# Products of constants ahead of TensorE's waits in a two-block transformer kernel

## The reference, cut to what matters

```
def first_block(x, c, ...):
    for i in range(2):
        sh1, sc1, g1, sh2, sc2, g2 = split(silu(c) @ ada_w[i] + ada_b[i], 6)
        h = rms_norm(x, norm_mix[i]) * (1 + sc1) + sh1
        x = x + g1 * (mla_mixer(h, ...) if i == 0 else gdn_mixer(h, ...))
        h = rms_norm(x, norm_ffn[i]) * (1 + sc2) + sh2
        x = x + g2 * (swiglu_ffn(h, ...) if i == 0 else moe_ffn(h, ...))
    return rms_norm(x, final_norm)

def second_block(x, ...):
    proj = rms_norm(x, norm_mix_pre) @ w_in
    ys = stack([rwkv7(proj), dilated_attention(proj), diff_attention(proj), conformer_conv(proj)])
    merged = sum_n(sigmoid(p_gate + gate_bias)[n] * (ys[n] @ w_branch[n]))
    x = x + rms_norm(merged @ w_out, norm_mix_post)
    h = rms_norm(x, norm_ffn_pre)
    return x + rms_norm((silu(h @ ffn_w_gate) * (h @ ffn_w_up)) @ ffn_w_down, norm_ffn_post)
```

## Time and profile before

| | |
|---|---|
| median of three runs | 3054.39 us |
| the profiled execution | 3055.6 us, its span 3054.3 us |
| TensorE busy | 2842.9 us (93%) |
| VectorE, ScalarE, GpSimd busy | 1724.3, 1246.3, 249.7 us |
| mean granted clock of TensorE | 0.973 |
| DMA | 387.94 MB, mean 127 GB/s |

### The profile page before, as it was taken

How to read it: one execution, slowest core, us unless ns; L and a number is a source line. 1 busy time by engine, 2 the same in 40 slices (tenths; PEclk the granted TensorE clock), 3 DMA queues, 4 the chain that set the end, 5 groups by cost and what they waited for, 6 DMA issues and landing times. The chain is left out here.

```text
span 3054.3 us, 40668 instructions
## 1 busy us (share of the span) xinstructions
PE 2842.9 (93%) x16535; PEld 2425.1 (79%) x16535; DVE 1724.3 (56%) x2989; ACT 1246.3 (41%) x2250; POOL 249.7 (8%) x224
## 2 busy tenths in 40 slices
PE   5988899999997989889999999899999999899998
PEld 4766788787886878789999997688778866678886
DVE  6666554445774867543468887543324396654344
ACT  2455432223433344423457776432223355432222
POOL 0000000000002543020000001112100002100000
PEclk8889999999999999989999999999999999999999
DMA  5232234422232111053579997211231203412321
GB/s 221 76 109 102 97 145 172 148 111 93 89 125 76 56 42 56 23 210 119 172 258 354 350 336 284 72 67 46 84 126 51 83 33 132 146 69 81 118 81 66
DMA packets 74418, 387.94 MB, mean 127 GB/s; under 512 B 8490, under 2 KB 10190, under 8 KB 42574
## 3 DMA queue, kind: packets, MB, share of 16 engines
q1 hardware_dynamic: 60816, 349.20, 31.3%
q10 hardware_dynamic: 10382, 26.07, 2.5%
q0 software_dynamic: 3024, 9.98, 0.9%
HBM read 368.43 MB, written 22.03 MB: 128 GB/s over the span
## 5 line engine op out<-in xcount | busy, mean ns | idle before, releaser
L342 DVE TENSOR_TENSOR wlo<-stage,whi 128x1024 fp32r<-128x1024 f32 (+4 forms) x524 | 533.8, 1059 | 352.2 <-ACT whi L354 351.6
L354 ACT ACTIVATE whi<-stage 128x1024 fp32r<-128x1024 f32 (+4 forms) x524 | 443.8, 896 | 210.7 <-PE ps L638 170.8
L638 PE MATMUL ps<-whi,mxhi 128*128 128x256 f32 x968 | 282.4, 292 | 11.0 <-DVE wlo L342 6.4
L638 PE MATMUL ps<-whi,mxlo 128*128 128x256 f32 x968 | 275.3, 284 | 0.0
L638 PE MATMUL ps<-wlo,mxhi 128*128 128x256 f32 x968 | 275.1, 284 | 0.0
L638 PE MATMUL ps<-bxhi,whi 128*128 128x512 f32 x480 | 199.7, 416 | 17.1 <-DVE bxlo L342 8.4
L638 PEld LDWEIGHTS ps<-whi,mxhi 128*128 128x128 f32 x968 | 186.5, 193 | 13.7 <-DVE wlo L342 5.6
L638 PE MATMUL ps<-bxhi,wlo 128*128 128x512 f32 x480 | 189.0, 394 | 0.0
L638 PE MATMUL ps<-bxlo,whi 128*128 128x512 f32 x480 | 188.5, 393 | 0.0
L638 PEld LDWEIGHTS ps<-wlo,mxhi 128*128 128x128 f32 x968 | 187.1, 193 | 0.0
L638 PEld LDWEIGHTS ps<-whi,mxlo 128*128 128x128 f32 x968 | 186.8, 193 | 0.0
(11 more groups left out here) (591 smaller groups left out, 6551.5 us busy)
## 6 DMA issues: line engine op xcount, KB each, us to landing
stage<-in_gu SPq DMA_DIRECT2D x91, 1024.0 KB, 5.8
more<-in_gu SPq DMA_DIRECT2D x41, 1024.0 KB, 7.0
stage<-in_ada SPq DMA_DIRECT2D x40, 1024.0 KB, 4.9
stage<-in_dn SPq DMA_DIRECT2D x36, 768.0 KB, 5.3
stage<-in_dn SPq DMA_DIRECT2D x32, 640.0 KB, 5.0
stage<-in_gin SPq DMA_DIRECT2D x16, 1024.0 KB, 4.8
stage<-in_gt SPq DMA_DIRECT2D x16, 1024.0 KB, 4.7
more<-in_dn SPq DMA_DIRECT2D x16, 640.0 KB, 5.1
```

What stands on the lines that cost most here:

```text
L342: return e.do.tensor_tensor(out, x, y, op)
L354: return e.do.activation(out, x, f, **kw)
L638: return self.p.do.matmul(out, lhsT, rhs, start=start, stop=stop, skip_group_check=True)
```

## The change

A new method `warm(n)` issues `n` plain fp32 products of the constant `ones` with the first 512 columns of the constants, into the bank that comes next in turn (after its last reader is done). Nobody reads them: the next real product into that bank starts a new sum. They are put ahead of 37 places in the executed program, 164 products in all. `pe_total` gets `ahead` and `behind`. At the query norm the wait for the whole table of constants moves ahead of the sum. The table `WARM` names heads and stages of the delta rule. `xs2`, `xs3`, `xs4`, `xs5` and `w2sum` are the sums of the norms ahead of the FFN, the delta rule, routing, the second block and that block's FFN.

```
+    def warm(self, n):
+        at = self.rot[self.turn % len(self.rot)]
+        before, self.prev[at] = self.prev[at], None
+        if before:
+            self.p.wait_ge(*[s(free(before)) for s in (self.A, self.V) if s.has(free(before))])
+        for _ in range(n):
+            self.mm(self.ps[at][:, :], self.c("ones"), self.cst_all[:, 0:512])
...
-    def pe_total(self, use, src, mark, ones=None, more=None):
+    def pe_total(self, use, src, mark, ones=None, more=None, ahead=0, behind=0):
+        self.warm(ahead)
...
         z.then_inc(*self.P.up(use))
+        self.warm(behind)
...
-        self.pe_total("sumq", L.tmp[0], V(("win", "sum", 3)))
         p.wait_ge(self.Dc("cst"))
+        self.pe_total("sumq", L.tmp[0], V(("win", "sum", 3)), ahead=9)
...
+        self.warm(6)
         for _ in self.pe_gemm("wo", "wo", range(4), L.X, lambda q: [V(("ot", "l", q))]):
...
+        self.pe_total("xs2", self.sq, self.V(("wo", "t", 6)), more=self.last_square, ahead=2, behind=8)
...
+        self.pe_total("xs3", self.sq, self.V(("f0", "t", 6)), more=self.last_square, ahead=3, behind=8)
...
+        self.warm(1)
         ps, vacant = self.take("bat")
...
+        self.warm(4)
         ps, vacant = self.take("gsum")
         p.wait_ge(self.V("decay"), *vacant)
         self.mm(ps[:, 0:32], self.c("tri"), L.sm(1))
         self.mm(ps[:, 32:64], self.c("ones"), L.sm(1)).then_inc(*P_.up("gsum"))
+        self.warm(5)
...
+    WARM = {(0, 2): 2, (0, 3): 7, (0, 4): 2, (1, 3): 3, (0, 6): 4, (0, 8): 4, (4, 3): 5, (4, 5): 3, (4, 8): 3, (3, 23): 4, (7, 26): 6}
...
+                self.warm(self.WARM.get((h, st), 0))
                 if st == 1:
...
+        self.pe_total("xs4", self.sq, V(("go", "t", 6)), more=self.last_square, ahead=2)
...
         for m in range(5):
+            self.warm(2)
             turn(m)
+        self.warm(3)
         ps, vacant = self.take("ranks")
...
         for m in range(5, 8):
             turn(m)
+        self.warm(7)
         self.pe_came(L, 0)
...
+        self.warm(8)
         self.pe_came(L, 1)
+        self.warm(2)
         gather(0, slice(0, 1))
         for t in range(2, tiles[0]):
             self.pe_came(L, t)
+        self.warm(3)
...
                         gather(0, slice(t, t + 1))
+                        self.warm((0, 1, 6, 1)[t])
...
+        self.pe_total("xs5", self.sq, self.V(("mo", "t", 6)), more=self.last_square, ahead=2, behind=18)
...
+        self.pe_total("w2sum", M.ring[0], self.V(("w2", "t", 6)), more=(M.ring[2], self.A(("w2", "q", 7))), ahead=3, behind=10)
```

More of the change, by code:

```diff
@@ L1324, in ffn0_pe @@
     def ffn0_pe(self, L, sums):
-        self.pe_total("xs2", self.sq, self.V(("wo", "t", 6)), more=self.last_square)
+        self.pe_total("xs2", self.sq, self.V(("wo", "t", 6)), more=self.last_square, ahead=2, behind=8)
         def between(e, j):
@@ L1511, in gdn_in_pe @@
         p, P_, A = self.p, self.P, self.A
-        self.pe_total("xs3", self.sq, self.V(("f0", "t", 6)), more=self.last_square)
+        self.pe_total("xs3", self.sq, self.V(("f0", "t", 6)), more=self.last_square, ahead=3, behind=8)
         for k, _ in enumerate(self.pe_gemm("gin", "gin", range(16), L.X, self.normed("n3"), lead=2)):
@@ L2055, in route_pe @@
         blocks = [slice(c * P, (c + 1) * P) for c in range(4)]
-        self.pe_total("xs4", self.sq, V(("go", "t", 6)), more=self.last_square)
+        self.pe_total("xs4", self.sq, V(("go", "t", 6)), more=self.last_square, ahead=2)
         for m in (5, 6, 7):
@@ L2652, in middle_pe @@
         self.p.wait_ge(*self.fence)
-        self.pe_total("xs5", self.sq, self.V(("mo", "t", 6)), more=self.last_square)
+        self.pe_total("xs5", self.sq, self.V(("mo", "t", 6)), more=self.last_square, ahead=2, behind=18)
     def middle_act(self, L):
@@ L3215, in merge_pe @@
             pass
-        self.pe_total("w2sum", M.ring[0], self.V(("w2", "t", 6)), more=(M.ring[2], self.A(("w2", "q", 7))))
+        self.pe_total("w2sum", M.ring[0], self.V(("w2", "t", 6)), more=(M.ring[2], self.A(("w2", "q", 7))), ahead=3, behind=10)
     def merge_act(self, L, M):
```

5 lines of the change are left out of this document (added).

## The result

The changed kernel takes 3095.57 us (median of 4, 3093.47 to 3097.15), the kernel before 3055.16 beside it (median of 4, 3051.13 to 3060.26): a ratio of 1.0134, 95% interval [1.0117, 1.0151]. The prediction had the direction right; its 3078 was 17 us short, and the time lies 3.6 us above the end of the wide range (3050 to 3092) and 5.6 above that of the forecast's own (3066 to 3090).

The account below looks back on a forecast made before the run. TensorE, busy 2842.9 of 3054.3 us, was taken to bound the kernel. Outside routing, 42.1 us of overruns less 22.4 of clock and 4 of later waits gave +15.7; routing +7.0; from 3055.6 to 3078, range 3066 to 3090 (wide 3050 to 3092).

Parts of the forecast that it names:

- A: Query norm: nine products ahead of the query sum, where no wait stands; 7.7 us overrun.
- B: Output projection: 6 products, 5.1 us, against a wait of 3.60 + 0.17; 1.35 us over.
- I: Second block's norm: 3 products ahead of its sum and 10 behind; 0.8 and 3.4 us over.
- C: FFN's norm: 2 products ahead fit their wait, 8 behind overrun theirs by 2.9 us.
- H: Branches' norm: 2 products ahead of the sum, 1.5 us over; 18 behind, 6.8 us over.
- D: Delta rule's norm: 3 products ahead about fill their wait, 8 behind overrun by 2.9 us.
- F: Delta rule's rounds: 12.2 us overruns, including empty places (4, 5), (3, 23), (7, 26) without waits; later waits return another 4.
- G: Routing: +7 us, from 8.3 + 2 + 0.7 of delays less 4 of clock; eight products assumed mostly inside a wait.
- third rival: More clock comes back: attention's two half-clock stretches go too, 13.7 us more won, 3065; chance 0.13.
- the first: Rival: a constant product takes one record's time, 0.43 us, so most fit their waits; 3030; chance 0.05.
- The second: Rival: later waits shrink and give back 38 of 57 us of overruns; 3042; chance 0.06.
- The fourth: Rival: no clock comes back, it falls in the waits left, overruns stand alone; 3113; chance 0.06.

Follow-up runs that it names:

- e0: The kernel before, unchanged, run and profiled once more: 3051.22 us (one run).
- e5: Kernel before with only the 43 products of the delta rule's rounds: 3064.46 us, ratio 1.0028 to the kernel before.
- e3: Changed kernel without the 22 products ahead of no wait (query norm, (4, 5), (3, 23), (7, 26)): 3090.09 us, ratio 1.0114 to the kernel before.
- e7: Changed kernel with counts cut to the waits, 54 products, none at the query norm or in routing: 3039.62 us, ratio 0.9954 to the kernel before.
- e6: Kernel before with only the products of routing and the experts' start: 3075.19 us, ratio 1.0069 to the kernel before.
- e2: Changed kernel without the eight products behind the expert flag's branch, ahead of the second pick: 3094.24 us, ratio 1.0131 to the kernel before.
- e8: Fitted kernel (e7) plus 3 products between the first pick and the flag's load: 3040.80 us, ratio 0.9959 to the kernel before.
- e1: Changed kernel with all counts halved, rounded down, 75 products instead of 164: 3056.74 us, ratio 1.0009 to the kernel before.
- e9: Fitted kernel (e7) plus one product ahead of each attention head's second values product: 3037.27 us, ratio 0.9948 to the kernel before.

## Why the prediction missed, by its steps

- **Price of a product and the clock at the filled places: right.** A product is 0.86 us, the half-clock stretches behind the filled norms are gone, and the mean clock is 0.987 where 0.985 was forecast. A, B, I are within 0.4 us, C within 0.2, but for 1.4 us by half-clock stretches in the FFN (493.5); H is 1.1 over, 0.7 of it a half-clock stretch further back in the branches. Of the clock as a whole the sum took 26.4 us and the rivals 33, which is its upper bound; 34 came, 7 of them in attention, where the sum had none.
- **D and the products ahead of xs4: mis-sized by 1 us each,** by a wait for a bank or for all engines that stands ahead of the products (0.78 and 0.72).
- **F, the rounds: the step that failed, 12 of the 18 us.** It is the term of the later waits. The forecast set 17.3 us of steps (12.2, and the 5.1 that it took off at the three empty places) against 9.1 that later waits (this 5.1 and another 4) and 8 that the clock give back. The trace has 20.2 us of steps; the clock gives back 8.3, as forecast; the later waits give back 2.2 in one piece and some 1 in small ones, not 9.1; and new half-clock stretches (1121.6, 1162.5) take 3.2. (The stretch at 1244.4 is not new: it stands at 1231 in the kernel before.) So some 6 us are waits that did not shrink, 3 are larger steps, and 3 are stretches of which e0 shows as much without a product. Changed kernel, PE:

```profile
1120.80 3.28 PE L647 MATMUL ps<-gwide 128*128 128x128 f32 x16 [2.05 <-POOL gwide L342]
...
1257.11 0.50 PE L647 MATMUL ps<-gyhi,whi 128*128 128x512 f32 x1 [0.81 <-DVE gylo L342]
```

  They are 1.96 and 0.81 us before: TensorE comes later and waits as long, so what GpSimd and VectorE do there comes later too; that it hangs on TensorE's own late results is the reading, not a run of its own. Only the third, of 2.05 us, went. And of the clock's gain at (0, 2) and (0, 4) 1.2 and 0.9 us ended in waits for the same chain. e5 (the same steps alone), e3 (7.8 us less without the empty places) and e7 (2.7 us of steps with 17 products) put the cost on the products in the rounds.
- **G, routing: the term of the eight products, 5 of its 6.6 us.** The forecast had 1.6 us over a wait of 5.0 (1.8 by its own numbers); the second pick came 6.9 us later, because the wait belongs to the branch. e6 repeats it, e2 shows the place without them, e8 shows the same wait filled for nothing from the other side. Another 1.1 us is the xs4 term above. The growth as a whole is good to some 3 us, by e0.
- **Attention** gave back 4.7 us in the profiled execution by a half-clock stretch less. The third rival named this as a mechanism; e0 shows that the kernel before can do it too, so it is no effect of the change that these runs establish. Without it the miss would have been larger; the forecast had named it as a sign of being wrong.
- **The rivals.** Two records a product rule out the first. The second needed 33 us of overruns to be given back, and the later waits gave back less than forecast. The fourth, no clock at all, is out by the stretches that are gone.
- **The choice itself.** The forecast took each place's clock as won only because nothing was left idle. e1 and e7 show that half of the products, with some of each wait left, win the same at the norms. So of the counts in the change the upper half buys nothing there and costs what is longer than the wait.

Open is why the low clock, gone from one place, comes at another with the same waits (e2, e3, e9), which makes the gains of the parts not add up. e0 shows that it also does so with no change at all, so these runs don't show that a filled place pushes it on.

The Trainium skill, "TensorE: Matmul & The Clock Gate", section "HAM oscillation — how this bites in real kernels", counts a low-clock stretch at half its length. The stretch of 6.8 us around the first product of the rounds would cost an estimated 3.4 us by it; the work in it became 2.4 us shorter in e1, and 1.2 of them were kept. So here even the work alone counts too much where a chain on other engines ends the wait.

## What to carry to other kernels

A product that is to keep the clock up must be shorter than the wait it stands in, and at the norms of this kernel half as many products did as well as all: fit them to what is left after the bank's wait, the wait for all engines and the branch, and leave every place without a wait empty. Read what ends a wait from the order in the engine's queue, not from the last semaphore: a product behind a flag's load and a branch fills nothing, one ahead of it is free. The clock's gain counts only as far as TensorE's own work ends the next wait. And take the same kernel's profile twice before a shift at one place is believed: here 3 to 5 us in three of the stages were the execution's own.

## What the runs showed of the hardware

- The compare-and-branch on the flag takes TensorE's sequencer 3.35 to 3.99 us in all fourteen traces, the others' 0.05 to 0.07 us. From VectorE's write of the flag to TensorE's next instruction behind load (0.49 us) and branch it is 4.0 to 4.6 us; products issued ahead run meanwhile (e8).
- Behind the norms the half-clock stretches were gone in e7 with four products (3.60 us) in a wait of 3.77 us, and in e1 and e7 with nine in one of 8.42, as with 8 and 18. In attention (13.7 to 37.5 us of work, where no product stands in it), rounds and routing they differ from execution to execution of the same program: 123.3 and 115.8 us of work at half clock in two profiles of the kernel before.
